# First delta head: the keys' SiLU and Gram matrix ahead of the last column groups, the values' convolution inside the head's first rounds, and the queries' products ahead of the turned values

## The reference

```python
u = jnp.dot(hmod, w_in)
qkv, z, b, a = jnp.split(u, ODD_SPLITS, axis=-1)
qkv_c, new_buf = causal_dwconv(qkv, conv_buf, conv_w)     # four taps per channel
qkv_c = jax.nn.silu(qkv_c)
q, k, v = jnp.split(qkv_c, (GDN_KW, 2 * GDN_KW), axis=-1)
q = l2_normalize(q) * (GDN_DK ** -0.5)                     # per head of 128
k = l2_normalize(k)
...
a_mat = jnp.einsum('nbhid,nbhjd->nbhij', k_beta, kc) * decay_strict
t_mat = unit_lower_inverse(a_mat, cb)                      # (I + a_mat)^-1 by repeated squaring
w = jnp.matmul(t_mat, k_beta * jnp.exp(gcum)[..., None])
u = jnp.matmul(t_mat, vc * bc[..., None])
qk = jnp.einsum('nbhid,nbhjd->nbhij', qc, kc) * decay_incl
... # a scan over the chunks carries the 128x128 state of the head
o = rms_norm(o, head_norm) * jax.nn.silu(z)
```

## Time and profile before

| | us |
|---|---|
| median of 3 runs | 1470.44 |
| lowest and highest | 1469.46, 1470.53 |
| the profiled execution's own time | 1466.97 |
| its span, first to last instruction | 1465.2 |
| busy: PE, DVE, ACT, POOL | 1419.8, 760.7, 409.8, 173.4 |
| granted TensorE clock, mean | 0.995 |

### The profile page before, as it was taken

How to read it: one execution, slowest core, us unless ns; L and a number is a source line. 1 busy time by engine, 2 the same in 40 slices (tenths; PEclk the granted TensorE clock), 3 DMA queues, 4 the chain that set the end, 5 groups by cost and what they waited for, 6 DMA issues and landing times.

```text
span 1465.2 us, 29810 instructions
## 1 busy us (share of the span) xinstructions
PE 1419.8 (97%) x12752; PEld 892.0 (61%) x12752; DVE 760.7 (52%) x1767; ACT 409.8 (28%) x1011; POOL 173.4 (12%) x342
## 2 busy tenths in 40 slices
PE   5999999999999999899999999999999999999998
PEld 3577765666644545566666666666666667665543
DVE  4737871444332444745747557465474574652244
ACT  5124431444411324112313222132221331322211
POOL 1122200000000110111201102011020120110111
PEclk9999999999999999999999999999999999999999
DMA  9520125000356011211110101111111111040033
GB/s 372 209 67 4 34 86 230 0 1 0 111 197 236 35 55 26 77 27 37 48 47 30 49 32 61 34 44 48 33 60 18 46 47 34 15 143 2 33 119 123
DMA packets 54583, 105.02 MB, mean 72 GB/s; under 512 B 34506, under 2 KB 37394, under 8 KB 51618
## 3 DMA queue, kind: packets, MB, share of 16 engines
q1 hardware_dynamic: 54452, 103.13, 20.4%
HBM read 88.25 MB, written 14.86 MB: 70 GB/s over the span
## 4 chain that ended last, share of the span: by engine, by line
PE 64%; DVE 5%; issue 1%; ACT 1%; DMA 0%; DVEq 0%; POOLq 0%; POOL 0%; ACTq 0%; SPq 0%
PE psum L802 62%; PE psum L805 2%; DVE mem L2251 1%; DVE mem L2268 1%; DVE mem L2483 1%; DVE mem L2282 1%; ACT mem L1661 0%; DVE mem L2420 0%; DVE mem L2261 0%; DVE mem L2429 0%; DMA mem<-eg_dram 0%; DVE mem L2248 0%; ACT mem L1627 0%; DVE mem L2362 0%; DVE mem L2438 0%
## 5 line engine op out<-in xcount | busy, mean ns | idle before, releaser
L802 PE MATMUL psum<-mem 32*32 32x32 f32 (+12 forms) x12144 | 1356.0, 297 | 23.6 <-issue 6.0
L802 PEld LDWEIGHTS psum<-mem 32*32 32x32 f32 (+4 forms) x12144 | 823.0, 137 | 517.5 <-issue 230.9
L2251 DVE SCALAR_TENSOR_TENSOR mem<-mem 128x384 f32<-128x384 f32 (+1 forms) x216 | 134.6, 623 | 2.7
L805 PE MATMUL psum<-mem 128*128 128x128 f32 (+1 forms) x608 | 86.0, 280 | 16.0 <-ACT mem L1454 10.9
L805 PEld LDWEIGHTS psum<-mem 128*128 128x128 f32 (+1 forms) x608 | 71.4, 145 | 49.2 <-issue 31.0
L1576 ACT ACTIVATE mem<-mem 128x256 f32<-128x256 f32 x72 | 35.5, 494 | 46.4 <-DVE mem L2125 46.4
L2165 DVE SCALAR_TENSOR_TENSOR mem<-psum,mem 128x1024 f32<-128x1024 f32 x12 | 15.2, 1269 | 60.4 <-POOL mem L684 60.4
L1726 ACT ACTIVATE mem<-mem 128x128 f32<-128x128 f32 x72 | 22.1, 307 | 82.2 <-DVE mem L2470 56.2
L2449 DVE COPY mem<-psum 128x128 f32<-128x128 f32 x64 | 18.7, 292 | 50.2 <-PE psum L802 49.8
L682 POOL TENSOR_SCALAR mem<-mem 128x1 f32<-128x1 f32 x17 | 3.7, 215 | 343.8 <-ACT mem L1597 343.8
L1633 ACT ACTIVATE mem<-psum 128x384 f32<-128x384 f32 x48 | 23.5, 490 | 73.5 <-PE psum L802 70.4
(11 more groups left out here) (220 smaller groups left out, 1006.1 us busy)
## 6 DMA issues: line engine op xcount, KB each, us to landing
mem<-modw SPq DMA_DIRECT2D x12, 2048.0 KB, 12.2
mem<-w SPq DMA_DIRECT2D x44, 512.0 KB, 3.4
mem<-x SPq DMA_DIRECT2D x1, 4608.0 KB, 18.4
x_dram<-mem SPq DMA_DIRECT2D x9, 512.0 KB, 2.6
mem<-row_dram SPq DMA_DIRECT2D x8, 576.0 KB, 3.7
mem<-x_dram SPq DMA_DIRECT2D x9, 512.0 KB, 3.7
mem<-wout SPq DMA_DIRECT2D x4, 1024.0 KB, 8.6
mem<-gs SPq DMA_DIRECT2D x8, 512.0 KB, 4.5
```

What stands on the lines that cost most here:

```text
L802: return pe.matmul(*a, **k)
L805: return pe.transpose(out, in_, ident[0:n, 0:n])
L2251: x = dve.scalar_tensor_tensor(cvm, U1[:, m, lo + j:hi + j], w, cvm, ALU.mult, ALU.add)
```

## The change

Seven edits, all in the second layer.

1. TensorE: for head 0, `gram_k(0)` and `turn_k(0)` stand after group 9 (`FRONT = 10`), ahead of group 10, instead of after group 10. `gram_q(0)` moves from there into `head(0)`, after the first slot's products.
2. DVE: for head 0, only groups 0 to 5 (keys and queries) are convolved ahead of the head; the keys' SiLU stands ahead of group 5, `front(0)` right behind group 5, then the two `gated`, the queries' SiLU and the keys' products.
3. DVE: the values' 12 taps stand in the first four slots of head 0, three in each (`VALUE_TAPS`), `norm_q(0)` after the first of them, the values' SiLU in slot 5.
4. ACT: the values' tanh moves from ahead of head 0 into its slot 4.
5. TensorE, all heads: in `extra(n)` the query-key products of blocks 0 to 3 and 4 to 7 change places with the transposed values, and the transposed sample block of the values moves from slot 1 to a new piece in slot 8.
6. DVE, all heads: `queries` and `values` change places to match; the last `queries` (third `eq_ready`) comes in round 4 instead of round 5.
7. The banks of these pieces change with them.

```diff
+FRONT = 10
+VALUE_TAPS = 3
...
                         transposes(3, 0, hi, "tk")
-                        pe.wait_ge(sem("s1_ready"), 3 * h + 3)
                         pe.wait_ge(sem("kd_ready"), 3 * h + 2)
-                        transposes(4, 2, (8,), "tv", 1)
                         pairs(4, 0, 1, (8,), "gq_mm", 2)
...
                     elif n == 4:
-                        pe.wait_ge(sem("vb_ready"), 3 * h + 1)
                         pe.wait_ge(sem("eq_ready"), 3 * h + 1)
-                        transposes(4, 2, lo, "tv")
+                        pairs(4, 0, 1, lo, "gq_mm")
                     elif n == 5:
                         pe.wait_ge(sem("umf_ready"), 2 * h + 1)
-                        transposes(2, 2, hi, "tv")
+                        pairs(2, 0, 1, hi, "gq_mm")
                     elif n == 6:
                         pe.wait_ge(sem("umf_ready"), 2 * h + 2)
-                        pairs(3, 0, 1, lo, "gq_mm")
+                        pe.wait_ge(sem("s1_ready"), 3 * h + 3)
+                        transposes(3, 2, lo, "tv")
+                    elif n == 7:
+                        pe.wait_ge(sem("eq_ready"), 3 * h + 2)
+                        transposes(4, 2, hi, "tv")
                     else:
-                        pe.wait_ge(sem("vb_ready"), 3 * h + 2)
-                        pairs(4, 0, 1, hi, "gq_mm")
+                        pe.wait_ge(sem("eq_ready"), 3 * h + 3)
+                        transposes(2, 2, (8,), "tv")
...
                     fill(h, 2 * r - 2, ahead)
+                    extra(2 * r - 2)
+                    if r == 1 and first:
+                        gram_q(0)
                     if r < 5:
-                        extra(2 * r - 2)
                         fill(h, 2 * r - 1, ahead)
                         extra(2 * r - 1)
...
             for j in range(BA_GROUPS * KT, GROUPS * KT - UPPER):
+                if j == FRONT * KT:
+                    gram_k(0)
+                    turn_k(0)
                 product(0, j)
-            gram_k(0)
-            turn_k(0)
-            gram_q(0)
...
+                if isinstance(h, int) and h == 0 and p == 4:
+                    silu_tanh(0, 2)
...
-            silu_tanh(0, 2)
...
+                if isinstance(h, int) and h == 0:
+                    for i in range(VALUE_TAPS * p, min(VALUE_TAPS * p + VALUE_TAPS, 3 * TAPS)):
+                        conv(0, 6 + i // TAPS, i % TAPS)
+                    if p == 5:
+                        silu(0, 2)
...
-                a, b, src = ((8, 9, four(4, 1, 1)), (0, 4, four(4)), (4, 8, four(2)))[n]
+                a, b, src = ((0, 4, four(3)), (4, 8, four(4)), (8, 9, four(2, 0, 1)))[n]
                 dve.wait_ge(sem("tv"), 3 * h + n + 1)
...
                     elif r == 2:
-                        values(h, 0)
                         queries(h, 0)
                     elif r == 3:
                         upper(h, 1)
                     elif r == 4:
-                        values(h, 2)
+                        queries(h, 2)
                     else:
-                        queries(h, 2)
+                        values(h, 1)
                     between(h, 2 * r - 2, ahead)
                     if r == 1:
+                        if isinstance(h, int) and h == 0:
+                            norm_q(0)
                         keys(h, 2)
                     elif r == 2:
                         upper(h, 0)
                     elif r == 3:
-                        values(h, 1)
+                        queries(h, 1)
                     elif r == 4:
-                        queries(h, 1)
+                        values(h, 0)
+                    else:
+                        values(h, 2)
...
-            for g in range(GROUPS - 1):
-                if g < GB:
-                    for j in range(TAPS):
-                        conv(0, g, j)
-                else:
-                    gated(0, g - GB)
+            for g in range(6):
+                if g == 5:
+                    silu(0, 0)
+                for j in range(TAPS):
+                    conv(0, g, j)
                 if g == 2:
                     exponents(0, 0, NT)
-            for m in range(2):
-                silu(0, m)
             front(0)
+            for g in range(GB, GROUPS - 1):
+                gated(0, g - GB)
+            silu(0, 1)
             keys(0, 0)
             keys(0, 1)
-            norm_q(0)
-            silu(0, 2)
```

More of the change, by code:

```diff
@@ L2336, in values @@
             def values(h, n):
-                a, b, src = ((8, 9, four(4, 1, 1)), (0, 4, four(4)), (4, 8, four(2)))[n]
+                a, b, src = ((0, 4, four(3)), (4, 8, four(4)), (8, 9, four(2, 0, 1)))[n]
                 dve.wait_ge(sem("tv"), 3 * h + n + 1)
                 if n == 0:
-                    dve.wait_ge(sem("gq_mm"), 3 * h + 1)
                     dve.wait_ge(sem("vs_ready"), h + 1)
@@ L2345, in queries @@
             def queries(h, n):
-                a, b, src = ((8, 9, four(4, 2, 1)), (0, 4, four(3)), (4, 8, four(4)))[n]
+                a, b, src = ((8, 9, four(4, 2, 1)), (0, 4, four(4)), (4, 8, four(2)))[n]
                 dve.wait_ge(sem("gq_mm"), 3 * h + n + 1)
```

## The result

The changed kernel takes 1458.86 us (median of 4 runs, 1456.57 to 1461.49) against 1470.49 us before: ratio 0.9922, 95% interval 0.9900 to 0.9943, or 11.6 us less. Timed again later, 1458.88 us against 1470.19, ratio 0.9927 (0.9911 to 0.9943). The prediction was 1461.2, range 1457.5 to 1466. Its profiled execution took 1461.49 us, the slowest of the four, while the one of before was faster than all its timed runs; so the spans differ by only 5.5 us. One execution, the profiled one of the order alone, ran in a slower state (1655.38 us, granted clock 0.85 over nearly its whole length); medians and ratios leave such executions out, and its trace isn't compared.

A forecast was written before the change was run, and what follows sets the result against it. TensorE, busy 1419.8 of 1465.2 us, was taken as the bound, so only its idle or half-clock time could be won. 5.62 + 3.3 + 0.6 - 0.2 - 0.1 = 9.2 us off 1470.44 gave 1461.2, range 1457.5 to 1466.

The forecast's parts named there:

- The idle time, 5.62 us: Entry of head 0: TensorE's two waits, 4.27 and 1.35 us, go if the new order keeps up.
- the walk through DVE and TensorE: Entry of head 0, step by step: round 1 near 619.0, round 2 near 625.5, against 634.2 before.
- The clock, 3.3 us: Entry of head 0: without idling, two half-clock stretches behind the waits go, half of 6.54 us.
- Two more alternations, 0.2: TensorE: two more switches between 384-column products and 32-wide tiles, taken to cost 0.1 us each.
- `norm_q`, 0.1: Before head 0's round 2: TensorE waits about 0.1 us for the queries' norm, bounds 0 and 0.6.
- the sum: Whole kernel: 5.62 + 3.3 + 0.6 - 0.2 - 0.1 = 9.2 us gained.
- The instruction stream, +0.6: Head 0's 1.16 us issue gap: half goes as transfers delaying a fetch move; bounds 1.2 gained, 1.9 to 3.6 lost.
- rival 4: Later heads: 256-instruction boundaries move against the bursts, one gap goes with its half clock: 1457.6 us; chance 0.07.
- Subtracting from the median: Final step: runs' median is 3.5 us above the profiled execution, so 9.2 is subtracted from 1470.44, giving 1461.2.
- 1 (the wait comes back): Head 0, rounds 2 to 4: DVE's taps make TensorE wait, 1466 or 1463.2 us; chance 0.20 with half clock staying.
- 2 (half clock stays): Entry of head 0: one half-clock stretch stays, 1.7 us less gained, 1463; chance 0.20 with the wait coming back.
- 3 (the row of decays hits round 5's burst): Seven heads: decays, issued a round earlier, delay instruction fetches, up to 23 us slower, 1484; chance 0.04.

The follow-up runs named there:

- the order alone: Kernel before with only the queries' products ahead of the turned values in all heads, head 0's entry as it was: 1466.8 us, ratio 0.9978.
- The taps back in the entry: Changed kernel with the values' twelve taps put back ahead of head 0: 1463.84 us, ratio 0.9957.
- the aligned kernel before: Kernel before with 33 waits for a long reached semaphore added in each of heads 1 to 6, making heads 2,560 instructions: 1462.60 us, ratio 0.9962.
- the order alone with such heads: Kernel of the order alone with 34 added waits in each of heads 1 to 6: 1459.92 us, ratio 0.9932.
- heads ended in the wrong place: Changed kernel with 34 waits in each of heads 1 to 6, plus 177 in head 0 ahead of its inverse: 1472.75 us, ratio 1.0033.
- 6 taps a slot: Changed kernel with six of the values' taps a slot in head 0 instead of three: 1459.29 us, ratio 0.9927.
- the kernel with the late history: Changed kernel with each head's three history transfers issued behind the row of decays, two rounds later: 1457.03 us, ratio 0.9913.

## Why the prediction was right, and where it wasn't

**The idle time, 5.62 us: right.** All of it went, and the walk through DVE and TensorE held to some tenths once it is shifted by group 9's later start (1.22): keys' SiLU done 0.6 us ahead of the Gram matrix, round 1 at 620.29 (walked 619.05 + 1.22 = 620.27), `gram_q` at 623.16 (walked 623.0), `norm_q` through at 626.93 (walked 626.8). One term of the walk is written wrongly: three taps stand as 2.0 us, but 0.41 and two of 0.65 are 1.7; they took 1.69 (624.09 to 625.78), and the walk's 625.55 goes with 1.7. The taps back in the entry bring 4.70 us of idling back.

**The clock, 3.3 us: right.** Both stretches of the earlier trace rows went, and the window from 607 to 640 is at 1.00. Two other profiles of the same entry (the aligned kernel before, and the order alone with such heads) have 10.2 us of half clock in a row. That isn't 5.1 us lost: TensorE stood still in part of it and was busy for 7.4 and 8.2 us, of which at most half was lost, 3.7 and 4.1; and from group 9 to round 2 they took 26.75 and 27.14 us, against 27.03 with the two stretches. So the price of the entry hardly depends on how many stretches there are. The mean clock (before 0.994 in the median run, the ten runs of the changed kernel 0.995 to 0.999, about 0.9977) counts idle time and all other stretches with it, and can't give a size for the entry.

**Two more alternations, 0.2, and `norm_q`, 0.1:** not told apart. From group 9 to round 2 it took 19.20 us, walked 625.4 + 0.1 - 607.13 = 18.4; the difference is the fetch gap of 0.84 that the walk didn't have. Without it TensorE would have come to round 2 at 626.71 and waited 0.2 us for `norm_q`. The entry's gain of 7.83 in the first pair is the 8.6 of the sum without its 0.6 for the fetches, less this gap.

**The instruction stream, +0.6: the step that failed, in its reason and in its sign.** Right was that the gaps are late fetches of blocks of 256. Wrong was "a fetch delayed by other transfers": with no other packet in flight the gap in head 3 was 1.80 us. What decides is where in the count of instructions the burst stands. The sign was wrong for the first profile: gaps went from 6.0 us in four to 7.4 in six, heads 1 to 6 lost 2.9 us more. The "luckier blocks" of rival 4 was the true mechanism, and here it went the other way. With most of it out, both kernels win (6.3 us, or 4.6 by the ratios, and 6.2 for the kernel before, where the two were timed together), and the change is worth 10.1 us, 0.9 more than the sum's 9.2. Of that the order has 2.7 by the same effect, which I had costed at nothing. So it is in part luck that the forecast came within 2.3 us of the median: the order alone won 3 to 4 us that the sum didn't have, and the gaps of the later heads went against it.

The Trainium skill, "Runtime: NRT & Kernel Launch", Instruction fetch mechanics, gives blocks of 256 instructions fetched while the current one runs, at a cost "mostly hidden". The traces agree on the blocks, and for most of them on the cost: of the 80 ends of blocks from 600 us on in the kernel before, four show a gap over 0.5 us. They disagree on what the few can add up to: in heads ended in the wrong place it is 20.2 us of 1472.75.

**Subtracting from the median.** The profiled execution of before was 3.5 us under its median, and I carried this over. With the profile after being its slowest, the two spans alone would have told of half the effect.

**The rivals.** 1 (the wait comes back): no; it needs 6 taps a slot, and then costs 1.54 us once. 2 (half clock stays): no. By the Trainium skill ("TensorE: Matmul & The Clock Gate", Part 1), which allows short gaps, the wait of 1.35 us ought to have cost no clock. That isn't decided: the stretch behind it went when it went, but it stood 3.5 us behind the end of a wait of 4.27, which went too, and a wait of 1.54 (six taps) had no half clock behind it. 3 (the row of decays hits round 5's burst): no gap stands there in the changed kernel. 4: above.

**What stays open.** Why a fetch starts when it does: in the kernel with the late history, with nothing else on the queues, it starts 0.4 us behind the first record of the block before in head 5 and 4.2 us in head 3. The longest, 5.4 and 5.9 us, stand in the last head, while other queues moved 0.9 MB; there a delay by transfers isn't ruled out. What fills the time between the fetch's landing and the first record. Why the record number is 193 and not 0. What decides whether half clock follows a gap: it did behind one of 1.78 (the last head of before) and not behind one of 2.19 (head 4 with six taps). The 7.4 us of medians for head 0 differ from the 8.6 predicted for it by less than such medians scatter; this isn't separated. Nor is it why the medians of the first pair are 11.6 us apart and the profiled spans 5.5.

## What to carry to other kernels

When a vector engine is late for a matrix engine at the start of a pipeline, sort its backlog by who waits for what, and put what nobody waits for into the slots behind; check with one larger setting (here six taps) how much slack the new place has. In a long unrolled program of small instructions, count the instructions of a period: if it isn't a multiple of 256, some periods can meet a late fetch in a burst, and an edit that adds or drops an instruction can move the time by some us; if it is a multiple, all periods share one place, good or bad (20.2 us lay between two such places here). Compare versions with the period padded, and read the gaps of each, or such luck is booked as the edit's merit. Here 34 idle instructions a head won 4.6 to 6.3 us, about half as much as the change.

## What the runs showed of the hardware

- A burst of 32-wide matmuls uses up 256 instructions in about 1 us; a fetch of a block took 0.9 to 1.7 us from 600 us on, and the first record of a block never came less than 2.15 us after its fetch started (1299 blocks). From 600 us on, the gaps of 0.4 to 3.9 us for which no engine or transfer is named all stand at ends of blocks.
- The same place in a block costs nothing in one head and 2.46 us in another (190 behind round 2's wait, heads 1 to 6 and the last).
- Waits for a semaphore long reached, put between products of 384 columns, cost nothing measurable: they make 204 instructions in a kernel whose heads take 94.61 us with and without.
- Half clock came behind some gaps of 1.8 to 2.5 us and not behind others of the same length, and the same gap had it in one execution of the changed kernel (head 3, 2.07) and not in the next (1.80).
- The entry with two idle waits took 27.03 us with 6.8 us of half clock, and 26.75 and 27.14 with 10.2: the third stretch, in part on idle time, made it no longer.
